# Two attention loops: earlier value sums, moved rotary work, value products ahead of the transposes in even steps

## The reference

```python
q = (cq @ w_uq).reshape(B, S, H, QK_NOPE + QK_ROPE)      # 64 + 32 a head
q_rope = rotate(q[..., QK_NOPE:], cos, sin)
k_nope = (ckv @ w_uk).reshape(B, S, H, QK_NOPE)
v = (ckv @ w_uv).reshape(B, S, H, V_DIM)
s = (q_nope . k_nope + q_rope . k_rope) * scale + t5_bias
o = softmax(s) . v
```

## Time and profile before

| what | us |
|---|---|
| median of 3 runs | 3153.94 (3151.17 to 3156.91) |
| the profiled execution | 3160.77 |
| its span | 3158.9 |
| PE busy | 2905.9 (92%) |
| DVE busy | 1456.9 (46%) |
| ACT busy | 929.8 (29%) |
| POOL busy | 992.8 (31%) |

### The profile page before, as it was taken

The page is one execution under the profiler, slowest core; times in us unless marked ns, Lnnn a source line. Parts: engine busy times, 40 slices in busy tenths (PEclk is TensorE's granted clock), DMA queues, the critical chain, the costliest instruction groups (busy, mean ns, idle before and its releaser), DMA issues.

```text
span 3158.9 us, 38916 instructions
## 1 busy us (share of the span) xinstructions
PE 2905.9 (92%) x14200; PEld 2385.2 (76%) x14200; DVE 1456.9 (46%) x2340; ACT 929.8 (29%) x1692; POOL 992.8 (31%) x766
## 2 busy tenths in 40 slices
PE   6899999978899999999986998999798999999997
PEld 3788887766588888888665777777685888888885
DVE  4455565551423323233446777777615323233235
ACT  2455544450200010000224666656502010100111
POOL 1333333433333233332411323222433233332331
PEclk8999999999899999999998999999999999999998
DMA  3423333323111111111203223232311111111111
GB/s 135 123 83 92 94 73 89 87 76 121 34 47 53 40 53 48 52 46 40 100 21 98 75 75 79 72 84 73 134 47 47 40 53 47 53 46 40 54 45 53
DMA packets 223834, 214.89 MB, mean 68 GB/s; under 512 B 41401, under 2 KB 187185, under 8 KB 222897
## 3 DMA queue, kind: packets, MB, share of 16 engines
q1 hardware_dynamic: 222570, 195.62, 22.4%
q10 hardware_dynamic: 1152, 17.83, 1.4%
HBM read 146.03 MB, written 21.23 MB: 53 GB/s over the span
## 4 chain that ended last, share of the span: by engine, by line
PE 76%; DVE 9%; ACT 7%; issue 3%; DMA 2%; SPq 1%; POOL 1%; ACTq 0%; DVEq 0%; POOLq 0%
PE psS L641 12%; PE psS L643 12%; PE psS L642 12%; PE psD L734 6%; PE psS L704 5%; PE psD L839 5%; PE psD L835 5%; PE psD L837 5%; PE psD L717 3%; ACT xT L994 3%; PE psD L768 2%; PE psD L769 2%; PE psD L770 2%; DVE xT L1231 2%; ACT pt L1005 2%
## 5 line engine op out<-in xcount | busy, mean ns | idle before, releaser
L641 PE MATMUL psS<-hT,W 128*128 128x512 f32 x1376 | 540.4, 393 | 28.5 <-POOL W L525 21.7
L642 PE MATMUL psS<-hT,W 128*128 128x512 f32 x1376 | 537.1, 390 | 0.0
L643 PE MATMUL psS<-hT,W 128*128 128x512 f32 x1376 | 537.0, 390 | 0.0
L559 POOL TENSOR_SCALAR xT<-xT,rden 128x1024 f32<-128x1024 f32 (+2 forms) x256 | 277.9, 1086 | 813.6 <-DVE rden L1239 813.6
L1247 DVE TENSOR_TENSOR pt<-psD,pt 128x512 fp32r<-128x512 f32 (+2 forms) x512 | 303.5, 633 | 240.2 <-ACT pt L1005 239.3
L523 POOL CAST W<-stage 128x1024 fp32r<-128x1024 f32 x108 | 112.4, 1041 | 942.7 <-PE psS L643 529.8
L1331 DVE TENSOR_TENSOR row<-psS,row 128x512 f32<-128x512 f32 x88 | 60.9, 692 | 739.9 <-PE psS L643 739.9
L1005 ACT ACTIVATE pt<-psD 128x512 fp32r<-128x512 f32 (+2 forms) x512 | 257.9, 555 | 283.8 <-PE psD L717 281.6
L641 PEld LDWEIGHTS psS<-hT,W 128*128 128x128 f32 x1376 | 259.4, 189 | 89.4 <-issue 25.4
L1341 DVE TENSOR_TENSOR xT<-psD,xT 128x512 f32<-128x512 f32 x352 | 237.6, 688 | 169.9 <-PE psD L839 169.8
L734 PE MATMUL psD<-pt,vv 128*128 128x256 f32 x1856 | 258.9, 292 | 56.9 <-DVE vv L1261 34.7
(11 more groups left out here) (160 smaller groups left out, 4655.7 us busy)
## 6 DMA issues: line engine op xcount, KB each, us to landing
stage<-in_w_gate SPq DMA_DIRECT2D x44, 512.0 KB, 3.8
stage<-in_w_up SPq DMA_DIRECT2D x44, 512.0 KB, 3.8
stage<-in_w_down SPq DMA_DIRECT2D x44, 512.0 KB, 3.5
kq<-split_x SPq DMA_DIRECT2D x132, 128.0 KB, 2.4
xT<-rel_c SPq DMA_DIRECT2D x16, 960.0 KB, 4.7
kq<-row SPq DMA_DIRECT2D x108, 128.0 KB, 2.4
stage<-in_w_even SPq DMA_DIRECT2D x24, 512.0 KB, 4.0
park<-xT ACTq DMA_DIRECT2D x2, 4096.0 KB, 14.0
```

The costliest lines, as they stand in the source:

```text
L559: pool.tensor_scalar(s, s, rden[:, t % 4:t % 4 + 1], 1.0, ALU.mult, ALU.mult).then_inc(S["normed"], 1)
L641: pe.matmul(o, wop(0, k), rhs(0, k, h), start=n == 0, stop=False)
L642: pe.matmul(o, wop(0, k), rhs(1, k, h), start=False, stop=False)
L643: mm = pe.matmul(o, wop(1, k), rhs(0, k, h), start=False, stop=n == len(ks) - 1)
```

## The change

1. sum early: keep_o_lo stands before exp on ScalarE, and sum_o before the reciprocal on VectorE, in both stages; keep_v_lo stands before bias_scores.
2. rotary moved: the three rotary instructions leave c_evict for c_rotate, which VectorE does last in the step after the product; their eviction comes two steps after the product (evicted_c). The order of the products becomes 2, 0, 1, 3, 4, 6, 5, 7, at steps 5, 7, 8, 9, 11, 12, 13, 14.
3. values ahead: in even steps, TensorE does values before turn_scores, in both stages.

SyncE's moves and the counts that are waited for follow the new order (left_c); which of the two staging buffers a product uses changes too (n = 0 and 3 take row2, the others split_x). No instruction is added or removed.

```diff
-STEPS_C = {0: 0, 1: 1, 3: 2, 5: 3, 7: 4, 8: 6, 9: 5, 10: 7}
+ORDER_C = (2, 0, 1, 3, 4, 6, 5, 7)
+STEPS_C = {5: 2, 7: 0, 8: 1, 9: 3, 11: 4, 12: 6, 13: 5, 14: 7}
+MOVED_C = (2, 0, 1, 3, 4, 5)
...
 def filler_c(t):
 
-    pair, x = (t - 6) // NSTEP + 1, (t - 6) % NSTEP
-    if t >= 6 and pair < PAIRS and x in STEPS_C:
+    pair, x = t // NSTEP + 1, t % NSTEP
+    if t >= 0 and pair < PAIRS and x in STEPS_C:
         return pair, STEPS_C[x]
     return None
 
 
+def evicted_c(t):
+
+    for back in (1, 2):
+        f = filler_c(t - back)
+        if f and (f[1] in (2, 3)) == (back == 2):
+            return f
+    return None
+
+
 def done_c(pair, n):
 
-    order = (0, 1, 2, 3, 4, 6, 5, 7) if pair else (2, 3, 0, 1, 4, 5, 6, 7)
-    return 6 * PAIRS + 8 * pair + order.index(n) + 1
-
-
-EV0_C, EV1_C = (4, 0, 8, 0, 12, 16), (0, 4, 0, 8, 0, 0)
+    return 6 * PAIRS + 8 * pair + ORDER_C.index(n) + 1
+
+
+def left_c(pair, n):
+
+    return 4 * PAIRS + 6 * pair + MOVED_C.index(n) + 1
+
+
+EV0_C, EV1_C = {2: 0, 1: 4, 4: 8, 5: 12}, {0: 0, 3: 4}
...
                     scores(0, t + 1, window_even, even_operands)
+                if t >= 4 and t % 2 == 0:
+                    values(0, (t - 4) // 2, window_even)
                 if 2 <= t < TILES + 2:
                     turn_scores(0, t - 2, window_even)
-                if t >= 4 and t % 2 == 0:
-                    values(0, (t - 4) // 2, window_even)
...
-                if n == (0 if pair else 2):
+                if n == 2:
                     pe.wait_ge(S["ws"], at("attn_c", "ws", 2 * pair + 2))
                 if pair:
-                    if n == 0:
+                    if n == 2:
                         pe.wait_ge(S["v_lo"], 2 * (PAIRS + pair))
-                    elif n < 5:
-                        pe.wait_ge(S["ev_lo"], 4 * PAIRS + 6 * pair + n)
-                    elif n == 6:
-                        pe.wait_ge(S["ev_lo"], 4 * PAIRS + 6 * pair + 5)
                     elif n == 5:
                         pe.wait_ge(S["v_row"], 2 * (PAIRS + pair) + 1)
                     else:
-                        pe.wait_ge(S["ev_lo"], 4 * PAIRS + 6 * pair + 6)
+                        pe.wait_ge(S["ev_lo"], left_c(pair, {0: 2, 1: 0, 3: 1, 4: 3, 6: 4, 7: 5}[n]))
...
                     scores(TILES, t + 1, window_c, c_operands)
+                if t >= 4 and t % 2 == 0:
+                    values(TILES, (t - 4) // 2, window_c)
                 if 2 <= t < TILES + 2:
                     turn_scores(TILES, t - 2, window_c)
-                if t >= 4 and t % 2 == 0:
-                    values(TILES, (t - 4) // 2, window_c)
...
                     keep_p_hi(0, t - 2, window_even)
+                if t >= 5 and t % 2 == 1:
+                    keep_o_lo(0, (t - 5) // 2)
                 if t < TILES:
                     exp_scores(0, t, window_even)
-                if t >= 5 and t % 2 == 1:
-                    keep_o_lo(0, (t - 5) // 2)
...
-                if n in (1, 3):
-                    sc.wait_ge(S["ev1"], 16 * (EV_EVEN + EV_C[1] * pair + EV1_C[n] - 4))
                     to = row2[:, 0, :]
                 else:
-                    sc.wait_ge(S["ev0"], 16 * (EV_EVEN + EV_C[0] * pair + EV0_C[n] - 4))
+                    sc.wait_ge(S["ev0"], 16 * (EV_EVEN + EV_C[0] * pair + EV0_C[n]))
...
-                if t and filler_c(t - 1):
-                    c_evict(*filler_c(t - 1))
+                if evicted_c(t):
+                    c_evict(*evicted_c(t))
...
+                if t >= 5 and t % 2 == 1:
+                    keep_o_lo(TILES, (t - 5) // 2)
                 if t < TILES:
                     exp_scores(TILES, t, window_c)
-                if t >= 5 and t % 2 == 1:
-                    keep_o_lo(TILES, (t - 5) // 2)
...
+                if step in (3, 4) and pair < PAIRS:
+                    keep_v_lo(0, pair, step - 3)
                 if t < TILES:
                     bias_scores(0, t, window_even, t < TILES // 2)
-                if step in (3, 4) and pair < PAIRS:
-                    keep_v_lo(0, pair, step - 3)
                 if 2 <= t < TILES + 2:
                     keep_p_lo(0, t - 2, window_even)
+                if t >= 5 and t % 2 == 1:
+                    sum_o(0, (t - 5) // 2)
                 if t < TILES:
                     reciprocals(0, t)
-                if t >= 5 and t % 2 == 1:
-                    sum_o(0, (t - 5) // 2)
...
             def c_evict(pair, n):
 
-                kind, h = n // 2, n % 2
-                cols, o = slice(h * HALF, (h + 1) * HALF), c_bank(pair, n)
-                if kind == 1:
-                    ve.wait_ge(S["prod"], done_c(pair, n))
-                    rq, other = o[0:HD, :], rstd[0:HD, cols]
-                    ve.scalar_tensor_tensor(other, o[HD:P, :], C_SCALE, xT[0:HD, SIN + h * HALF:SIN + (h + 1) * HALF],
-                                            ALU.mult, ALU.mult).then_inc(S["r_rot"], 1)
-                    ve.scalar_tensor_tensor(rq, rq, C_SCALE, cos_t[0:HD, cols], ALU.mult, ALU.mult)\
-                        .then_inc(S["r_rot"], 1)
-                    ve.wait_ge(S["r_rot"], 6 * pair + 3 * h + 2)
-                    ve.tensor_tensor(rq, rq, other, ALU.add).then_inc(S["r_rot"], 1)
-                b = row2 if n in (1, 3) else split_x[:, :, :]
-                ve.wait_ge(S["ev_hi"], 4 * PAIRS + 6 * pair + n + 1)
+                kind, o = n // 2, c_bank(pair, n)
+                b = row2 if n in EV1_C else split_x[:, :, :]
+                ve.wait_ge(S["ev_hi"], left_c(pair, n))
...
+            def c_rotate(pair, n):
+
+                h, o = n % 2, c_bank(pair, n)
+                ve.wait_ge(S["prod"], done_c(pair, n))
+                rq, other = o[0:HD, :], rstd[0:HD, cols]
+                ve.scalar_tensor_tensor(other, o[HD:P, :], C_SCALE, xT[0:HD, SIN + h * HALF:SIN + (h + 1) * HALF],
+                                        ALU.mult, ALU.mult).then_inc(S["r_rot"], 1)
+                ve.scalar_tensor_tensor(rq, rq, C_SCALE, cos_t[0:HD, cols], ALU.mult, ALU.mult)\
+                    .then_inc(S["r_rot"], 1)
+                ve.wait_ge(S["r_rot"], 6 * pair + 3 * h + 2)
+                ve.tensor_tensor(rq, rq, other, ALU.add).then_inc(S["r_rot"], 1)
...
+                if step in (3, 4) and pair < PAIRS:
+                    keep_v_lo(TILES, pair, step - 3)
                 if t < TILES:
                     bias_scores(TILES, t, window_c, True)
-                if t and filler_c(t - 1) and filler_c(t - 1)[1] < 6:
-                    c_evict(*filler_c(t - 1))
-                if step in (3, 4) and pair < PAIRS:
-                    keep_v_lo(TILES, pair, step - 3)
+                if evicted_c(t) and evicted_c(t)[1] < 6:
+                    c_evict(*evicted_c(t))
                 if 2 <= t < TILES + 2:
                     keep_p_lo(TILES, t - 2, window_c)
+                if t >= 5 and t % 2 == 1:
+                    sum_o(TILES, (t - 5) // 2)
                 if t < TILES:
                     reciprocals(TILES, t)
-                if t >= 5 and t % 2 == 1:
-                    sum_o(TILES, (t - 5) // 2)
+                if t and filler_c(t - 1) and filler_c(t - 1)[1] in (2, 3):
+                    c_rotate(*filler_c(t - 1))
```

More of the change, by code:

```diff
@@ L449, in move_c @@
                 kind, h = n // 2, n % 2
[L450 to L453, removed]
+                cols = slice(h * HALF, (h + 1) * HALF)
+                b, sem = (row2, S["ev1"]) if n in EV1_C else (split_x[:, :, :], S["ev0"])
+                sp.wait_ge(S["ev_lo"], left_c(pair, n))
                 for e in range(2):
@@ L470, in _ @@
             rel_table(rel_c, TILES, 1, 1)
-            for n in range(6):
+            for n in MOVED_C:
                 move_c(0, n)
@@ L477, in _ @@
                     store_head(TILES, (t - 6) // 2)
-                if t and filler_c(t - 1) and filler_c(t - 1)[1] < 6:
-                    move_c(*filler_c(t - 1))
+                if evicted_c(t) and evicted_c(t)[1] < 6:
+                    move_c(*evicted_c(t))
                 if pair < PAIRS - 2 and step == 5:
@@ L901, in c_operands @@
                 return [(qh, kh), (qh, kl), (ql, kh)]
-            for n in (2, 3, 0, 1, 4, 5, 6, 7):
+            for n in ORDER_C:
                 c_product(0, n)
@@ L1134, in c_evict @@
                     return
-                if n in (1, 3):
-                    sc.wait_ge(S["ev1"], 16 * (EV_EVEN + EV_C[1] * pair + EV1_C[n] - 4))
+                if n in EV1_C:
+                    sc.wait_ge(S["ev1"], 16 * (EV_EVEN + EV_C[1] * pair + EV1_C[n]))
                     to = row2[:, 0, :]
                 else:
-                    sc.wait_ge(S["ev0"], 16 * (EV_EVEN + EV_C[0] * pair + EV0_C[n] - 4))
+                    sc.wait_ge(S["ev0"], 16 * (EV_EVEN + EV_C[0] * pair + EV0_C[n]))
                     to = split_x[:, 0, :]
@@ L1146, in c_evict @@
                     sc.activation(flipped(to), blocks(o), ACT.Copy, scale=C_SCALE).then_inc(S["ev_hi"], 1)
-            for n in range(8):
```

(10 more changed lines are left out.)

## The result

The changed kernel takes **3257.5 us**, the median of 4 runs (3254.92 to 3258.85), against 3155.43 for the kernel before in 4 runs beside it (3151.17 to 3161.78): a ratio of 1.032 [1.030, 1.034]. The profiled execution has a span of 3256.3, against 3158.9: 97.4 us to find. Lines behind the change's first hunks stand 14 lower in the new file: scores L704 are L718 now, transposes L717 are L731, values L734 are L748, the latent product L894 is L904, bias L1231 is L1241.

A forecast was written before the change was run, and what follows sets the result against it. TensorE, losing time to waits, was taken to bound the kernel. Profiled 3160.8 + 55 (stage C without clock) + 14 (clock) + 16 (even stage) = 3246, less 6.8 for the median: 3239 us, range 3205 to 3265.

The forecast's parts named there:

- the walk of the prediction: Stage C: strides of one pair added from values to values, 78.6 us against 71.5 before.
- The loop of part 3: Stage C steps without filler: values, transposes, p_hi, exp, bias, p_lo, sum_o take 8.03 us per two steps, against 7.29.
- what it gives part 3 takes: Stage C: the early sum alone would save waits, but with values ahead its gain is already counted in the loop's 8.03 us.
- most of the 0.58 waits: Stage C, value products waiting for sum_o: part 1 alone would save most of these 0.58 us waits.
- The even stage: Stage before C: a loss of +16 us in all, bounds -5 to +30, split over three kinds of pairs.
- Part 2's wait: Stage C steps 7 and 11: products n = 0 and n = 4 wait 4.2 us for the bank, twice a pair.
- Transfers: Stage C step 15: waits of 2.0 to 2.3 us for moved operands go; the new order of moves costs nothing.
- The clock: Stage C: half-clock stretches behind the 14 waits cost 1.0 us each, +14 us, bounds 0 to 47.
- the clock follows every wait: Rival, stage C: each of the 14 waits costs 3.4 us of low clock, total 3273 us; chance 0.10.
- The reading by which the clock term would be 0: Values straight behind scores keep TensorE's matmuls back to back, so no clock loss; total 14 us lower.
- half the stall: Rival, steps 7 and 11: TensorE is late anyway, each wait costs 2 us instead of 4.2, total 3194 us; chance 0.15.
- The faster rival: Rival: evictions come in time, early sum and removed transfer wait decide, 21 us less, 3133 us; chance 0.11.

The follow-up runs named there:

- e8_parts13: Kernel before with parts 1 and 3, the rotary work in its old place: 3195.35 us, 1.012 of the kernel before.
- e3_part1: Kernel before with part 1 alone (early sum and early value split, both stages): 3113.98 us, 0.986 of the kernel before.
- e2_part3: Kernel before with part 3 alone (values ahead of the transposes in even steps): 3246.23 us, 1.027 of the kernel before.
- e1_parts12: Changed kernel with part 3 undone in both stages, so parts 1 and 2 remain: 3127.09 us, 0.990 of the kernel before.
- e7_half_ahead: Changed kernel with each value product cut in two, eight matmuls ahead of the transposes and eight behind: 3189.49 us, 1.010 of the kernel before.
- e4_rot_early: Changed kernel with the rotation between bias and p_lo and its eviction ahead of the next bias: 3194.45 us, 1.011 of the kernel before.
- e5_t_first_rot_early: Changed kernel with part 3 undone, rotation between bias and p_lo, its eviction ahead of the next bias: 3091.52 us, 0.979 of the kernel before.
- e6_even_only: Changed kernel with part 3 undone in stage C and kept in the even stage: 3161.78 us, 1.002 of the kernel before.

## Why the prediction was right, step by step

Strides of one pair, from the starts of value products in the changed kernel's trace, against the walk of the prediction. The clock's part is what the same matmuls took longer than in neighbouring steps at full clock:

| steps | predicted | measured | of it clock | without |
|---|---|---|---|---|
| 0 to 2 | 8.0 | 7.94 | | 7.94 |
| 2 to 4 | 10.3 | 10.01 | | 10.01 |
| 4 to 6 | 8.5 | 8.61 | | 8.61 |
| 6 to 8 | 11.3 | 11.91 | 0.73 | 11.18 |
| 8 to 10 | 10.5 | 11.23 | 0.80 | 10.43 |
| 10 to 12 | 12.7 | 15.06 | 2.52 | 12.54 |
| 12 to 14 | 9.2 | 9.20 | | 9.20 |
| 14 to 0 | 8.1 | 7.97 | | 7.97 |
| sum | 78.6 | 81.9 | 4.05 | 77.9 |

- **The loop of part 3** was right: 8.03 us worked out, 7.94 measured, and one turn of it in the changed kernel's last pair takes the way that the prediction named:

```profile
2322.54 2.15 PE L748 MATMUL psD<-pt,vv 128*128 128x256 f32 x16
...
2324.53 1.03 PE L731 MATMUL psD<-flip_t,xT 128*128 128x128 f32 x8
2325.22 1.08 ACT L1015 ACTIVATE pt<-psD 128x512 fp32r<-128x512 f32 x2 [3.07 <-PE psD L731]
...
2326.19 1.15 ACT L1004 ACTIVATE xT<-xT,mneg 128x1024 f32<-128x1024 f32 x1
...
2327.58 1.23 DVE L1241 CUSTOM_DVE_ANT_0 xT<-psS,xT 128x1024 f32<-128x1024 f32 x1
...
2328.73 1.28 DVE L1257 TENSOR_TENSOR pt<-psD,pt 128x512 fp32r<-128x512 f32 x2
...
2328.87 1.66 PE L718 MATMUL psS<-kq 96*128 96x512 f32 x6 [1.02 <-DVE mneg L1241]
...
2329.93 0.41 DVE L1265 TENSOR_TENSOR o_out<-psD,o_lo 64x256 f32<-64x256 f32 x1
...
2330.49 2.15 PE L748 MATMUL psD<-pt,vv 128*128 128x256 f32 x16
```

  Values, transposes, p_hi, exp, bias, p_lo and sum_o start 1.99, 0.69, 0.97, 1.39, 1.15, 1.20 and 0.56 us before their successors, 7.95 together. In this turn the view of waits shows only the scores' wait for the bias (1.02 here), which is a second way round that is nearly as long: these scores end at about 2328.87 + 1.38 = 2330.25, and the values come 0.24 later, 0.56 behind the start of sum_o, as in the earlier trace rows. So the sum closes the loop, by 0.24 us.

- **Part 1 inside the loop**: as a net sum, "what it gives part 3 takes" held, since parts 1 and 3 together (e8_parts13) are 38 us slower than before. But part 1's gain is not lost beside part 3: it is 45 us alone (e3_part1) and about 51 with part 3 in place (e2_part3 to e8_parts13). In the stride from step 4 to step 6 of the last pair: 7.29 before, 6.46 with part 1, 8.55 with part 3, 7.95 with both. About 18 of the 51 us lie in the even stage (stage C starts at 1714.1 instead of 1732.3), and in stage C the stretches at half clock go from twelve (48 us) to four (14 us). Alone, the size in stage C was near: "most of the 0.58 waits" and at most 1.14 of the wait for v_lo come to about 4 us a pair, and the pair fell by 3.9 on average. The even stage, where I had looked only for losses, gained about 15 (stage C starts at 1684.3 instead of 1699.2).
- **Part 2's wait**: 4.2 predicted, 3.74 measured, fourteen times. The chain behind the transposes was 7.06 instead of 7.2, and TensorE's work before the wait was 0.34 longer than the 2.98 I had taken. The statement that part 3 makes it worse by one value product is shown by e1_parts12 (1.84) and e7_half_ahead (2.8). n = 3 waited 1.0 instead of 1.3.
- **Transfers**: the waits of step 15 went and none came elsewhere, as costed. The Trainium skill (Perfetto Trace Analysis, Matmuls) has independent groups of matmuls rotate through different PSUM banks. No run here gives the fillers a second bank; but e4_rot_early, which frees the one bank 2.9 us sooner by VectorE's order alone, is 63 us faster, so the traces agree that the wait for the one bank costs.
- **The clock** is the mis-sized term. I took 1.0 us for each of fourteen waits, 14 in all; it is 4.05 a pair, 28 in all, within the bounds of 0 and 47. The condition of the rival "the clock follows every wait" came true, fourteen times in fourteen; its price of 3.4 did not, for the mean is 2.0 a wait. The reading by which the clock term would be 0 did not come true either. Step by step: each pair has a stretch of 3.41 us at half clock just behind the first wait and one of 6.83 that begins 1.3 us before the second wait ends (in the first of the seven pairs both are 6.83). Behind the second a filler of nine takes 4.01 instead of 2.18, and the scores 2.07 instead of 1.38:

```profile
2019.29 0.80 PE L904 MATMUL psD<-hT,W 128*128 128x512 f32 x1 [3.74 <-DVE row L1395]
...
2023.30 2.23 PE L718 MATMUL psS<-hT 96*128 96x512 f32 x6
2025.37 0.89 PE L748 MATMUL psD<-pt,vv 128*128 128x256 f32 x6
```

  I had argued that TensorE has slack there because ScalarE and VectorE are behind. But a filler of nine, scores and values stand in its queue at that point, 5.5 us of work, and they are the path. The bound of 3.4 a wait was not reached by the second wait (2.52) and is far from the first (1.53, the 0.73 and 0.80 of its stretch).
- **The even stage**: +19.3, predicted +16. Of the four plain pairs with 1024 keys the first three lost little (+0.7, -0.1, -0.1) and the fourth 4.8, the neighbourhood pairs 0.4, 2.4 and 3.6, and the last pair with the change of stage 8.0. As a sum it was near, but it did not fall pair by pair as I had split it, and 4.6 us of it can be scatter: that the sum is near is partly luck.
- **Sum**: stage C without the clock's part in its pairs 70.2 - 28 + 9.8 = 52 (predicted 55; the tail behind the last pair is 4.8 of it, where I had 1), clock 28 (14), even stage 19.3 (16), elsewhere -1.9: 97 against 85. Of the 18.5 us between 3239 and 3257.5 these 12 are terms of the sum; some 5.5 more come from the executions, since the profiled one before was 6.8 us over the median, which the forecast took off, and that of the changed kernel only 1.4.

Of the rivals, "half the stall" did not come in the changed kernel, where the wait was 3.74; waits of about half the size came only where an experiment cut them (1.84 in e1_parts12). The faster rival, where only gains are left, is what e5_t_first_rot_early shows, at 3092 instead of 3133: it needs the eviction to be in time, which takes both the values behind the transposes and the rotation away from the reciprocal. What stays open is why the clock fell in a pair where it did: of the fourteen waits of 1.84 us in e1_parts12 five had a stretch at half clock behind them, and no run here varies one wait alone.

## What to carry to other kernels

An order on one engine's queue is judged by the loop that it closes over all engines: before moving work ahead of the instruction that feeds another engine, add up the way round until its own result comes back, and compare with the work that is left to fill it. Two edits that lengthen the same way round can cost more than their sum (49 us more, here), so run them apart: one edit of three was worth 45 us, one -13 us on top of it, one -81 to -130 us, and the second turned to a gain of some 20 us when the rotation and its eviction moved to earlier places in VectorE's order.

## What the runs showed of the hardware

Each of the changed kernel's fourteen waits of 3.74 us on TensorE had a stretch at the low clock level (granted 0.50, 1.2 GHz) at its end. In the last six pairs of seven it was 3.41 us long and began 1.3 us behind the first wait; at the second wait it was 6.83 us long and began 1.3 us before the wait was over. In the first pair both were 6.83. The stretches cost 4.05 us a pair on top of the waits' 7.5, so here the stall has to be priced at half as much again.

Shorter waits before the fillers had such a stretch less often: of fourteen waits of 2.8 us eight (e7_half_ahead), of fourteen of 1.84 us five (e1_parts12) and four (e6_even_only), of fourteen of 0.83 none (e4_rot_early, whose two stretches start at a value product behind a wait of 1.05 for v_lo). A long wait is not needed: in the last pair of e2_part3 the value product at 2305.72 took 3.65 us, with only a wait of 0.56 right before it and one of 1.02 before the scores ahead of it.

TensorE's busy time rises with the stall, by 35 us here, because slow matmuls count as busy: a higher busy time is no sign of more work done.
